# A network of transformer blocks on one core: up-projections of the feed-forward blocks in wide matmuls

## The reference

```python
D_MODEL, SEQ, D_FF = 1024, 256, 2816

def swiglu(h, w_up, w_down):
    gate, up = jnp.split(h @ w_up, 2, axis=-1)
    return (jax.nn.silu(gate) * up) @ w_down

x = x + 0.5 * swiglu(rmsnorm(x, n1), wu1, wd1)     # four times, around the mixers of the first block
h = h + _swiglu(hn, ffn_w_gate, ffn_w_up, ffn_w_down)    # once, in the second block (factor 1)
```

## Time and profile before

| what | value |
|---|---|
| median of 3 runs | 2244.11 us (2240.51 to 2244.17) |
| the profiled execution | 2237.9 us |
| its span, first to last instruction | 2236.1 us |
| mean granted TensorE clock | 0.977 |
| PE busy | 2108.6 us, 94% |
| DVE busy | 1516.4 us, 68% |
| ACT busy | 1070.7 us, 48% |
| three groups of matmuls of the up steps | 500.0, 498.8, 498.8 us |

### The profile page before, as it was taken

One profiled execution on the slowest core, in us unless ns is written; L12 is line 12 of the kernel. 1 busy time (PEld: TensorE's weight loads), 2 busy tenths in 40 slices (PEclk: granted clock), 3 DMA queues, 4 the chain that ended last, 5 costly groups with the idle time before them and its releaser, 6 DMA issues.

```text
span 2236.1 us, 35373 instructions
## 1 busy us (share of the span) xinstructions
PE 2108.6 (94%) x13755; PEld 1893.8 (85%) x13755; DVE 1516.4 (68%) x2023; ACT 1070.7 (48%) x1509; POOL 452.9 (20%) x205
## 2 busy tenths in 40 slices
PE   7999988999999998999998998999987899999997
PEld 7999977999999996899986787999975778888886
DVE  5566886665666666565658546665676568888887
ACT  4434543534533444534353224334445367777775
POOL 2222222222223230222220232222230000000000
PEclk9999999999999999999999999999998889999998
DMA  8555411555555541455542003555450368888885
GB/s 327 196 178 173 166 57 57 188 180 187 170 193 178 193 151 57 145 194 188 182 149 84 1 1 132 196 178 190 151 198 7 146 234 330 316 326 328 331 327 197
DMA packets 73403, 401.54 MB, mean 180 GB/s; under 512 B 8257, under 2 KB 8385, under 8 KB 41153
## 3 DMA queue, kind: packets, MB, share of 16 engines
q1 hardware_dynamic: 72848, 398.27, 50.7%
q10 hardware_dynamic: 432, 1.57, 0.2%
HBM read 398.76 MB, written 1.05 MB: 179 GB/s over the span
## 4 chain that ended last, share of the span: by engine, by line
PE 81%; DVE 11%; ACT 3%; issue 2%; POOL 1%; PEld 1%; DMA 0%; DVEq 0%; SPq 0%; ACTq 0%; PEldq 0%
PE psum L302 24%; PE psum L303 23%; PE psum L304 23%; DVE w_lo L286 2%; PE psum L899 2%; PE psum L312 2%; PE psum L889 1%; PE psum L2365 1%; ACT w_hi L279 1%; POOL w_lo L292 1%; DVE r_e L2052 1%; PE psum L880 1%; PE psum L1637 0%; PE psum L2378 0%; DVE y_lo L2622 0%
## 5 line engine op out<-in xcount | busy, mean ns | idle before, releaser
L286 DVE TENSOR_TENSOR w_lo<-ring,w_hi 128x1024 fp32r<-128x1024 f32 x498 | 769.0, 1574 | 317.9 <-ACT w_hi L279 316.0
L279 ACT ACTIVATE w_hi<-ring 128x1024 fp32r<-128x1024 f32 x744 | 739.2, 1051 | 386.0 <-PE psum L304 207.5
L292 POOL TENSOR_TENSOR w_lo<-ring,w_hi 128x1024 fp32r<-128x1024 f32 x160 | 401.8, 2511 | 1146.8 <-ACT w_hi L279 1146.8
L302 PE MATMUL psum<-fT_hi,w_hi 128*128 128x256 f32 x1760 | 500.0, 284 | 10.4 <-DVE w_lo L286 10.1
L304 PE MATMUL psum<-fT_hi,w_lo 128*128 128x256 f32 x1760 | 498.8, 283 | 0.0
L303 PE MATMUL psum<-fT_lo,w_hi 128*128 128x256 f32 x1760 | 498.8, 283 | 0.0
L302 PEld LDWEIGHTS psum<-fT_hi,w_hi 128*128 128x128 f32 x1760 | 338.3, 192 | 17.2 <-issue 6.9
L303 PEld LDWEIGHTS psum<-fT_lo,w_hi 128*128 128x128 f32 x1760 | 338.3, 192 | 3.7
L302 PE MATMUL psum<-w_hi,hT_hi 128*128 128x384 f32 (+4 forms) x896 | 321.9, 359 | 17.5 <-issue 7.9
L304 PEld LDWEIGHTS psum<-fT_hi,w_lo 128*128 128x128 f32 x1760 | 338.2, 192 | 0.0
L304 PE MATMUL psum<-w_hi,hT_lo 128*128 128x384 f32 (+4 forms) x896 | 310.9, 347 | 0.0
(11 more groups left out here) (461 smaller groups left out, 2535.6 us busy)
## 6 DMA issues: line engine op xcount, KB each, us to landing
ring<-in_stream SPq DMA_DIRECT2D x249, 1024.0 KB, 5.0
ring<-in_stream SPq DMA_DIRECT2D x248, 512.0 KB, 4.1
tables<-in_tables SPq DMA_DIRECT2D x1, 2453.0 KB, 20.5
gain_row<-in_gains ACTq DMA_DIRECT2D x3, 512.0 KB, 3.7
rows<-in_rows SPq DMA_DIRECT2D x1, 1288.0 KB, 24.5
X<-in_x SPq DMA_DIRECT2D x1, 1024.0 KB, 5.0
result<-X SPq DMA_DIRECT2D x2, 512.0 KB, 2.7
columns<-in_columns SPq DMA_DIRECT2D x1, 993.0 KB, 15.2
```

The costliest lines, as they stand in the source:

```text
L279: act.activation(part(w_hi, g, i), ring[:, k, i * PART:(i + 1) * PART], ACT.Copy) \
L286: dve.tensor_tensor(part(w_lo, g, i), ring[:, k, i * PART:(i + 1) * PART], part(w_hi, g, i).bitcast(F32), ALU.subtract) \
L292: pool.tensor_tensor(part(w_lo, g, 2), ring[:, k, 2 * PART:STEP], part(w_hi, g, 2).bitcast(F32), ALU.subtract) \
L302: pe.matmul(out_, w[0], x[0], start=first, stop=False, skip_group_check=True)
```

## The change

The input's halves move into one tensor `fT`, in which `x_hi` and `x_lo` of one k lie side by side, 512 columns in all. In up(s), each `w_hi` tile is multiplied with these 512 columns at once, for all k and o. Then come all products of `w_lo` with `x_hi`, of 256 columns. Gate and up part now have a bank each, banks 4 and 5 for even steps and 6 and 7 for odd ones. The first half of a bank holds hi by hi plus lo by hi; the second half holds `w_hi` by `x_lo`. So the halves have to be added: ACT copies both second halves to SBUF (`up_sums`), and DVE adds the first halves to that. The multiplications after it read `up_sums` in place of PSUM. The row of factors goes to bank 3, as bank 7 is taken.

```diff
-            fT_hi, fT_lo = (take(n, [P, KT, SEQ], F32R) for n in ("fT_hi", "fT_lo"))
+            fT = take("fT", [P, KT, 2, SEQ], F32R)
+            fT_hi, fT_lo = fT[:, :, 0, :], fT[:, :, 1, :]
+            up_sums = take("up_sums", [P, 2, 2, SEQ])
...
+        def up_half(s, half):
+
+            return psum[:, 4 + 2 * (s % 2):6 + 2 * (s % 2), half * SEQ:(half + 1) * SEQ]
...
                 if peeled and after_mixer(at):
-                    settle_bank(pe, 4 + s)
+                    for o in range(2):
+                        settle_bank(pe, 4 + 2 * s + o)
...
                         if after_mixer(at):
-                            settle_bank(pe, 7)
-                        row_tensor(pe, at, psum[:, 7, :])
+                            settle_bank(pe, 3)
+                        row_tensor(pe, at, psum[:, 3, :])
                     for o in range(2):
-
-                        ins = three_passes(pe, psum[:, 4 + s % 2, o * SEQ:(o + 1) * SEQ], [x[:, o, k, :] for x in w],
-                                           [x[:, k, :] for x in (fT_hi, fT_lo)], k == 0 and o == 0, k == KT - 1)
+                        pe.matmul(psum[:, 4 + 2 * (s % 2) + o, :], w[0][:, o, k, :], fT[:, k, :, :].rearrange("p a c -> p (a c)"),
+                                  start=k == 0, stop=False, skip_group_check=True)
+                for k in range(KT):
+                    for o in range(2):
+                        ins = pe.matmul(psum[:, 4 + 2 * (s % 2) + o, 0:SEQ], w[1][:, o, k, :], fT_hi[:, k, :],
+                                        start=False, stop=k == KT - 1, skip_group_check=True)
                 ins.then_inc(ffn_up_ready, 1)
...
+                act.wait_ge(ffn_up_ready, f0 + sv + 1)
+                act.activation(up_sums[:, s % 2, :, :], up_half(s, 1), ACT.Copy).then_inc(ffn_extra_kept, 1)
                 act.wait_ge(ffn_scaled, f0 + sv + 1)
...
-                dve.wait_ge(ffn_up_ready, f0 + sv + 1)
-                dve.tensor_tensor(silu[:, s % 2, :], psum[:, 4 + s % 2, 0:SEQ], rstd_row[:, :], ALU.mult).then_inc(ffn_scaled, 1)
+                sums = up_sums[:, s % 2, :, :]
+                dve.wait_ge(ffn_extra_kept, f0 + sv + 1)
+                dve.tensor_tensor(sums, up_half(s, 0), sums, ALU.add).then_inc(ffn_summed, 1)
+                dve.wait_ge(ffn_summed, f0 + sv + 1)
+                dve.tensor_tensor(silu[:, s % 2, :], sums[:, 0, :], rstd_row[:, :], ALU.mult).then_inc(ffn_scaled, 1)
...
-                dve.tensor_tensor(gated[:, s % 2, :], silu[:, s % 2, :], psum[:, 4 + s % 2, SEQ:2 * SEQ], ALU.mult).then_inc(ffn_gated, 1)
+                dve.tensor_tensor(gated[:, s % 2, :], silu[:, s % 2, :], sums[:, 1, :], ALU.mult).then_inc(ffn_gated, 1)
```

More of the change, by code:

```diff
@@ L202, in network_kernel @@
         ffn_up_ready = sem("ffn_up_ready")
+        ffn_extra_kept = sem("ffn_extra_kept")
+        ffn_summed = sem("ffn_summed")
         ffn_scaled = sem("ffn_scaled")
@@ L781, in step @@
                     stats_vector(dve, at, factor)
-                    row_vector(dve, at, psum[:, 7, :])
-                dve.wait_ge(ffn_up_ready, f0 + sv + 1)
-                dve.tensor_tensor(silu[:, s % 2, :], psum[:, 4 + s % 2, 0:SEQ], rstd_row[:, :], ALU.mult).then_inc(ffn_scaled, 1)
+                    row_vector(dve, at, psum[:, 3, :])
+                sums = up_sums[:, s % 2, :, :]
[3 more added lines that the diff above has]
+                dve.tensor_tensor(silu[:, s % 2, :], sums[:, 0, :], rstd_row[:, :], ALU.mult).then_inc(ffn_scaled, 1)
                 dve.wait_ge(ffn_silu_ready, f0 + sv + 1)
```

## The result

Changed kernel: 2222.66 us, median of 4 runs (2220.13 to 2225.91); kernel before beside it: 2243.23 us (2240.51 to 2244.17). The ratio is 0.9911 [0.9894, 0.9928]: 0.9% less time. The forecast was 2233.6 us and, at the best, 2227. The direction was right, the gain was too small. A second set of runs, with 21 of the kernel before (median 2240.47 us, 2236.94 to 2244.44) and 5 of the changed one, gives 0.9921 [0.9906, 0.9935]: 17.8 us less (14.6 to 21). The profiled executions, one of each kernel, took 2237.9 us (span 2236.1) and 2222.65 us (span 2220.8), 15.3 us apart, which lies inside the second interval. The three figures differ mainly in the kernel before: the 2237.9 us of its profiled execution are 2.6 us under the median of the 21.

The account below looks back on a forecast made before the run. PE, busy all the time in the feed-forward loops, was taken as the bound. Loop -18.0, block ends +6.0 and starts +1.5 gave -10.5 us, so 2244.1 became 2233.6 us; range 2227 to 2242 us.

Parts of the forecast that it names:

- part 1: PE in the loop: 16 fewer matmuls per up step save 0.18 us a step, -18.0 us (16.9 to 19.3).
- the last line: End of the sum: runs' median lies 6.2 us above the profiled execution, so 2244.1 - 10.5 = 2233.6 us.
- Rival A: Wide matmuls after narrow ones are slower, so the loop saves only 7.4 us: 2244 us, chance 0.10.
- Part 2: In the loop: ACT's copy (0.60 us) and DVE's addition (0.69 us) are hidden and cost nothing.
- Part 3: End of each block: copy and addition delay the last down step; five blocks cost +6.0 us (3.5 to 8.5).
- Part 4: Block starts: -0.5 us at two together, +2.0 us at three after mixers; +1.5 us in all (-1 to +4).
- B: The fixed cost isn't saved with the instruction, so the loop gains nothing: 2251.6 us, chance 0.04.
- C: In up steps, each change of bank costs PE 13 ns more, 41.6 us in all: 2275 us, chance 0.05.
- D: The chain through the addition bounds the loop at 8.6 us instead of 8.32: 2262 us, chance 0.02.
- E: Block ends cost less than forecast and starts lose nothing: 2228 us; chance 0.79 together with the forecast.

## Why the prediction was wrong

Two terms of the sum were mis-sized: the saving of part 1, by 3.3 us, and the last line, which turns the profile's time into that of the runs, by 6.2 us. The mechanism of the change was right.

**Part 1: the spacing of a wide matmul.** It took that spacing, 0.2275 or 0.229 us, from down steps, and settled on 0.18 us a step. The saving is 8.50 - 8.287 = 0.213 us, 21.3 us instead of 18.0, outside its bounds of 16.9 to 19.3. Cut in two again, the wide ones give all of it back. An undisturbed wide matmul takes 0.2267. The 0.229 is the mean of a down step that follows narrow matmuls: its first half is slower, 0.2317, and its last half at 0.2267 (the lines of 1005.09 to 1007.84 above). The wide matmuls of up follow those of down, so they never meet that. The 0.2275 of rows 6 follows wide ones and has no slow half; it is too high by the view's rounding and by its last matmul (0.232), which a transpose follows. That is small, but times 16 it is 0.013 us of a saving of 0.2. Of the 0.033 us a step that part 1 missed, 0.014 came from leaning from 0.194 (0.19 in the text) towards the 0.17 that 0.229 gives, 0.013 from 0.2275, and the rest from the narrow ones and from rounding. Rival A had seen the slower start and drew the wrong conclusion from it: up now changes width in every step, but from wide to narrow. The turn from narrow to wide still comes once a step, at down, as before.

The fixed part, beyond the columns at 2.4 GHz, is the same for both widths away from a turn: 0.1200 - 0.1067 = 13.3 ns for a narrow matmul and 0.2267 - 0.2133 = 13.3 for a wide one, and 16 x 13.3 ns is the 0.213 us saved. The Trainium skill, "TensorE: Matmul & The Clock Gate", section "Wait — 56ns, not 53.3ns?", has about 2.5 ns; by that the change would have been worth 4 us in the loop, an estimate. The trace disagrees with its 21.3 us, as the prediction held. Why the two differ no run here shows; here every matmul has a weight load of its own.

**Part 2** was right: copy 0.597 and addition 0.690 us, PE without a pause in the loop, ACT still waiting 0.57 us for the buffer behind the silu (forecast 0.5), and the chain at 7.27 us for an estimated 7.3, if with two more additions it sets the whole period.

**Part 3** was right: the last down step begins 3.82 us after the one before it, forecast 3.84, and is 0.12 longer: 1.07 + 0.12 = 1.19 us a block, 6.0 in all.

**Part 4** was right in sum: up(2) came earlier by 0.24 us against the block's start behind a feed-forward block (forecast 0.27), and later by 0.62 after a mixer (forecast 0.65), so +1.4 us for +1.5. The gap at k = 6 was 0.79 us, not 1.1, and the wait before up(2) 1.00, not 1.1 to 1.3. For the start of the program the term can't be judged: up(2) begins there at 32.66 us in the one trace of the changed kernel and at 33.91 in the other.

**Sum.** With part 1 as measured: -21.3 + 6.0 + 1.4 = -13.9, and the blocks show -13.9. Another 1.4 us came outside them, which I had put at nothing; the code there is the same, and the two traces of the changed kernel differ there by up to 0.9 us in a single stretch.

**From the profile to the runs.** The larger part of the miss is the last line of the sum. I carried the 6.2 us by which the median of three runs lay above the profiled execution over to the changed kernel. Of these, 3.6 were chance in three runs (2244.11 against 2240.47 of 21), and 2.6 chance in the profiled execution; the changed kernel's profiled execution lies at its median. The 21 executions of the kernel before show what the chance hangs together with: the five with a granted clock of 0.973 took 2243.8 to 2244.4 us, the five with 0.978 or 0.979 took 2236.9 to 2239.1. So 2233.6 was too high by 3.3 of part 1, 1.4 outside the blocks and 6.2 of this: 10.9 us, which is the miss. The range was too narrow because it held only the bounds of the terms, none for the baseline.

**Rivals.** A: the price of a change of width exists, 0.03 us a turn when the groups are long, but isn't new in the changed kernel. B is refuted by the period, C by the run with eight matmuls in a row into one bank, D by the period and by the runs with more additions. E named the near edge, for the wrong reason: the ends cost what was forecast.

## What to carry to other kernels

When PE is busy without a pause, count its matmuls: each has its fixed cost, so one with twice the columns saves it, and extra work on engines with slack is free only where a next step covers it. The first and last steps of a loop have no such cover; do them in the short-chain form (here the runs were 12 us faster than with the change alone, 9.2 of them in the blocks). Take an instruction's spacing from neighbours of the same shape, read to more places than the answer needs, and put the baseline's own scatter into the range.

## What the hardware showed that I had not expected

- fp32 matmuls of 256 and 512 columns in turn cost 7 ns a pair more than in groups (0.3536 against 0.3462 us); after a turn from narrow to wide five matmuls are slower, by 0.03 us in all.
- Beyond its columns at 2.4 GHz a matmul costs 13.3 ns at either width (0.1200 and 0.2267 us), each with a weight load of its own.
- Going to another PSUM bank with every matmul costs nothing: 3.63 us for 16 wide ones, and the same when eight in a row share one.
- After a wait of 1.51 us PE went on at 2.4 GHz (a down step of 2.83 us). After one of 3.88 us, in a kernel whose loops also had short pauses, the matmuls of a whole down step stood 0.427 us apart, as at 1.2 GHz; at the other four ends, with waits of 3.86 to 3.92 us, the down steps were 1.4 to 2.3 us longer.
- The places where the clock is lowered differ between two executions of one kernel: 892 to 897 us had 0.66 in one and 1.00 in the other, at no cost; in another kernel a lowered clock on busy matmuls came with 1.6 us.
